# A hybrid decoder step on Trainium2: where the first output projection step stands beside the sample attention's tail

## The reference, cut to what matters

```
o   = softmax(q_lat . past_c + q_rope . past_r) . past_c      # per sample token and head: a latent of 256
a   = einsum('bshr,rhv->bshv', o, w_uv)                       # 8 heads of 64: 512 values a token
g   = spatial_gate(u, v, w_s, b_s)                            # 512 values a token
x   = x + concat(rmsnorm(a) * g_mla, rmsnorm(g) * g_gmlp) @ w_out
```

## Time and profile before

| | |
|---|---|
| time before, median of 3 runs | 1296.98 us (1295.57 to 1297.92) |
| the profiled execution's own time | 1297.65 us |
| its span | 1295.9 us |
| PE busy | 1259.2 us, 97% |
| PE weight loads busy | 1181.9 us, 91% |
| DVE busy | 903.9 us, 70% |
| ACT busy | 592.9 us, 46% |
| POOL busy | 559.1 us, 43% |
| granted PE clock, mean | 0.993 |

### The profile page before, as it was taken

How to read it: one execution, slowest core, us unless ns; L and a number is a source line. 1 busy time by engine, 2 the same in 40 slices (tenths; PEclk the granted TensorE clock), 3 DMA queues, 4 the chain that set the end, 5 groups by cost and what they waited for, 6 DMA issues and landing times.

```text
span 1295.9 us, 24153 instructions
## 1 busy us (share of the span) xinstructions
PE 1259.2 (97%) x9110; PEld 1181.9 (91%) x9110; DVE 903.9 (70%) x1470; ACT 592.9 (46%) x1222; POOL 559.1 (43%) x567
## 2 busy tenths in 40 slices
PE   9999999999999989999999999999999999999997
PEld 7888998888787559999899999999999999999987
DVE  4983167777765436188955787676776679899986
ACT  7433235665655324124454444444444544444462
POOL 0732344354431226751265977878877800000000
PEclk9999999999998999999999999999999999999998
DMA  9421102000027435630221222222222397868503
GB/s 324 144 63 34 49 5 76 5 21 1 17 70 269 156 145 201 204 119 26 84 83 60 92 74 78 90 70 92 85 75 92 122 339 262 295 196 267 164 1 139
DMA packets 70405, 151.93 MB, mean 117 GB/s; under 512 B 9138, under 2 KB 16690, under 8 KB 69842
## 3 DMA queue, kind: packets, MB, share of 16 engines
q1 hardware_dynamic: 70290, 150.39, 34.5%
HBM read 127.80 MB, written 22.56 MB: 116 GB/s over the span
## 4 chain that ended last, share of the span: by engine, by line
PE 79%; DVE 9%; issue 4%; ACT 3%; POOL 2%; DMA 2%; SPq 0%; DVEq 0%; POOLq 0%; ACTq 0%
PE ps L1196 23%; PE ps L1198 23%; PE ps L1197 23%; PE ps L1442 2%; DMA araw<-in_w_dn 1%; PE ps L1500 1%; PE ps L1454 1%; PE ps L1562 1%; PE ps L1455 1%; ACT pTH L1880 1%; DVE nmx L2735 1%; POOL chunk L1165 1%; DVE pTL L2752 1%; PE ps L1527 1%; DVE prob L2729 1%
## 5 line engine op out<-in xcount | busy, mean ns | idle before, releaser
L1165 POOL TENSOR_TENSOR chunk<-wraw,chunk 128x256 fp32r<-128x256 f32 x193 | 163.2, 869 | 100.0 <-ACT chunk L1880 99.9
L1196 PE MATMUL ps<-bHL,aHL 128*128 128x272 f32 x616 | 178.3, 289 | 2.7 <-DVE bHL L3283 2.7
L1198 PE MATMUL ps<-bHL,aHL 128*128 128x272 f32 x616 | 177.2, 288 | 0.0
L1197 PE MATMUL ps<-bHL,aHL 128*128 128x272 f32 x616 | 177.1, 288 | 0.0
L1165 POOL TENSOR_TENSOR chunk<-wsum,chunk 128x256 fp32r<-128x256 f32 x134 | 115.8, 881 | 26.7 <-ACT chunk L1880 26.5
L1880 ACT ACTIVATE chunk<-wraw 128x256 fp32r<-128x256 f32 x193 | 74.9, 412 | 104.7 <-PE ps L1198 38.4
L1196 PEld LDWEIGHTS ps<-bHL,aHL 128*128 128x128 f32 x616 | 116.0, 188 | 3.9 <-DVE bHL L3283 3.8
L1197 PEld LDWEIGHTS ps<-bHL,aHL 128*128 128x128 f32 x616 | 116.0, 188 | 0.0
L1198 PEld LDWEIGHTS ps<-bHL,aHL 128*128 128x128 f32 x616 | 115.9, 188 | 0.0
L1188 POOL TENSOR_TENSOR rt<-ms,mhalf 128x3 f32<-128x3 f32 (+1 forms) x3 | 4.4, 1463 | 246.1 <-DVE ms L3373 246.1
L1102 POOL TENSOR_TENSOR prob<-prob,rsm 128x128 f32<-128x128 f32 (+5 forms) x48 | 49.6, 1042 | 78.2 <-DVE rsm L2724 78.2
(11 more groups left out here) (494 smaller groups left out, 4605.1 us busy)
## 6 DMA issues: line engine op xcount, KB each, us to landing
araw<-in_w_dn SPq DMA_DIRECT2D x121, 256.0 KB, 3.2
wraw<-in_w_gu SPq DMA_DIRECT2D x44, 512.0 KB, 3.8
cp<-in_cache SPq DMA_DIRECT2D x64, 272.0 KB, 4.7
ab<-acts SPq DMA_DIRECT2D x34, 272.0 KB, 3.8
raw<-in_w_out SPq DMA_DIRECT2D x16, 512.0 KB, 4.3
acts<-bufC SPq DMA_DIRECT2D x22, 272.0 KB, 2.1
xt<-in_x_tok SPq DMA_DIRECT2D x9, 512.0 KB, 5.6
x<-x2s SPq DMA_DIRECT2D x8, 544.0 KB, 6.0
```

The lines of the kernel that those rows point to most:

```text
L1165: pool.tensor_tensor(x[:, 1, :], source_of(i, step), x[:, 0, :], ALU.subtract).then_inc(cw_lo, 1)
L1196: nc.tensor.matmul(out, wh, xh, start=start, stop=False, skip_group_check=onto)
L1197: nc.tensor.matmul(out, wh, xl, start=False, stop=False, skip_group_check=onto)
L1198: return nc.tensor.matmul(out, wl, xh, start=False, stop=stop, skip_group_check=onto)
```

## The change

PE's order becomes `sample_product(3)`, q = 0, `sample_latents(3)`, the matmuls with `uvr` (now the function `sample_values`), q = 1, the sum of squares, q = 2, the spread, q = 3. `sample_latents(g)` writes bank g and no longer g % 3. On ACT `mixed_high(0)` moves ahead of `move_sample_product(3)`; on DVE `mixed_low(0)` moves ahead of `move_latents(3)`. q = 0 waits for the copies of group 0 out of bank 0 (`o4`), and the wait for `a4_e`, which guards bank 2, stays at q = 2. No instruction that computes is added or taken away, and no transfer is moved.

```diff
@@ PE
             def sample_latents(g):
                 pe.wait_ge(o4_tok, g + 1)
-                if g == 3:
-                    pe.wait_ge(o4, KC)
                 for r in range(KC):
-                    last = nc.tensor.transpose(ps[:, g % 3, P * r:P * r + P], otok[:, g, P * r:P * r + P],
+                    last = nc.tensor.transpose(ps[:, g, P * r:P * r + P], otok[:, g, P * r:P * r + P],
                                                ident[:, :])
...
             sample_product(3)
-            sample_latents(3)
-            pe.wait_ge(o4, KC * DUOS)
-            pe.wait_ge(ld_uv_x, 16)
-            for h in range(H):
...
-            last.then_inc(a4, 1)
+            def sample_values():
+                pe.wait_ge(o4, KC * DUOS)
+                pe.wait_ge(ld_uv_x, 16)
+                for h in range(H):
...
+                last.then_inc(a4, 1)
@@ PE, the loop over OUT_STEPS, ahead of the step's matmuls
                 if q >= 4:
                     pe.wait_ge(w_free, q - 3)
+                elif q == 0:
+                    pe.wait_ge(o4, KC)
                 elif q == 1:
+                    sample_latents(3)
+                    sample_values()
+                elif q == 2:
                     sum_squares(J_N3 + NC - 1, 6, sqm, KG, CH[NC - 1][1])
-                elif q == 2:
                     pe.wait_ge(a4_e, 1)
@@ ACT
             move_sample_turned(3)
-            move_sample_product(3)
...
             mixed_high(0)
+            move_sample_product(3)
             act.wait_ge(a4, 1)
@@ DVE
             move_latents(2)
-            move_latents(3)
...
             mixed_low(0, range(2 * KG))
+            move_latents(3)
             mixed_low(1, range(2 * KG))
```

More of the change, by code:

```diff
@@ L1616, in _ @@
             sample_product(3)
-            sample_latents(3)
-            pe.wait_ge(o4, KC * DUOS)
-            pe.wait_ge(ld_uv_x, 16)
-            for h in range(H):
[L1621 to L1624, removed]
-            last.then_inc(a4, 1)
+            def sample_values():
+                pe.wait_ge(o4, KC * DUOS)
+                pe.wait_ge(ld_uv_x, 16)
+                for h in range(H):
+                    out = ps[VH * (h % 2):VH * (h % 2) + VH, 2, NS * (h // 2):NS * (h // 2) + NS]
+                    for r in range(KC):
+                        last = nc.tensor.matmul(out, uvr[:, r, VH * h:VH * h + VH], olat[:, r, NS * h:NS * h + NS],
+                                                start=r == 0, stop=r == KC - 1)
+                last.then_inc(a4, 1)
             def row_sum(bank, sources, i, o):
@@ L2828, in move_latents @@
                     out = olat[:, r, :].rearrange("p (h b t) -> p b h t", h=H, b=NB)[:, 2 * g:2 * g + 2, :, :]
-                    nc.vector.tensor_copy(out, ps[:, g % 3, P * r:P * r + P].rearrange(
+                    nc.vector.tensor_copy(out, ps[:, g, P * r:P * r + P].rearrange(
                         "p (b h t) -> p b h t", b=2, h=H)).then_inc(o4, 1)
```

## The result

| | before | changed |
|---|---|---|
| median, 7 runs each | 1296.98 us (1295.27 to 1299.54) | 1302.71 us (1301.76 to 1304.44) |
| profiled execution, own time | 1297.65 | 1304.13 |
| span | 1295.9 | 1302.4 |

The ratio is 1.0044, with a 95% interval of 1.0034 to 1.0053: slower by 5.7 us, where 4.0 was forecast. The ratios on record are not the quotients of the medians; here the two differ most.

The account below looks back on a forecast made before the run. PE, busy 97% of the span, was taken to bound the kernel. PE's order -0.65 + 0.53 + 2.78 = +2.66 plus the clock's 1.4 gave +4.1 on 1296.98, forecast 1301.0 us, range 1298.7 to 1303.0.

Parts of the forecast that it names:

- The wait for the product's copy goes: PE after the last sample product: its standing for ACT's copy disappears because q = 0 stands in its place, -0.65 us.
- q = 0 waits for its low operand: PE at q = 0: DVE's mixed_low(0) is held by POOL's weight splits, +0.53 us, bounds 0 and +1.2.
- q = 1 must wait for its operand: PE after the uvr matmuls: mixed_high(1) stands behind a4, copy and squares on ACT, +2.78 us, bounds 2.5 and 3.2.
- The clock: PE around q = 1: granted clock likelier than not falls to 1.2 GHz, +1.4 us, bounds 0 and 5.1.
- Rival (a): PE around q = 1: the clock does not fall; +2.7 us, 1299.7; chance 0.30.
- The sum of squares moves behind q = 1: PE ahead of q = 2: the sum of squares' 1.89 us is paid either way, so 0.
- The means, the power and the spread: DVE's means and power after the sum of squares: done 498.05, PE asks at 498.2; only just in time, up to +0.3.
- (b): Part of the slip is absorbed or overrated at q = 1's operand, DVE's hold or later PE waits; 1298.3; chance 0.12.
- (c): Faster: q = 0 hides ACT's copy and nothing waits at q = 1, as block 1's operand is ready; 1296.3; chance 0.06.
- (d): q = 0 is held until DVE is done at 484.5 and hides nothing; 1301.8; inside the forecast case's 0.52.

Follow-up runs that it names:

- e2: Changed kernel, but POOL splits the weights of i = 1 only after mixed_low(0) is done: 1301.13 us, ratio 1.0033 to the kernel before.
- e3: Changed kernel, but on ACT mixed_high(1) stands ahead of the wait for a4: 1297.74 us, ratio 1.0007 to the kernel before.
- e7: Changed kernel with 10 spare products by ones on PE after the uvr matmuls, ahead of q = 1: 1300.26 us, ratio 1.0028 to the kernel before.
- e6: Kernel before with only the ACT and DVE moves of mixed_high(0) and mixed_low(0), PE's order as before: 1302.04 us, ratio 1.0043 to the kernel before.
- e4: Changed kernel, but the sum of squares stands between the uvr matmuls and q = 1: 1299.50 us, ratio 1.0021 to the kernel before.
- after_again: Changed kernel run once more, unaltered, for its median and a second trace: 1300.67 us against 1297.22, ratio 1.0037 to the kernel before.
- e1: Changed kernel with 15 spare products by ones on PE after the uvr matmuls, ahead of q = 1: 1300.48 us, ratio 1.0027 to the kernel before.
- e8_latents_inside: Changed kernel, mixed_high(1) ahead of a4's wait, POOL's second split behind mixed_low(0), last group's transposes inside q = 0: 1295.12 us, ratio 0.9985 to before.

## Why the prediction was right

**The direction and the main mechanism were right, step by step.** Predicted and measured, in the changed kernel's first trace, from the start of the last product:

| step | predicted | measured |
|---|---|---|
| product to q = 0 | 3.60 | 3.60 |
| q = 0, partly held by DVE | 3.65 | 3.81 |
| transposes to `uvr` matmuls | 1.02 | 0.96 |
| `uvr` matmuls to q = 1 | 3.91 | 3.92 |
| q = 1 | 3.28 + 1.4 | 4.59 |
| sum of squares to q = 2 | 1.90 | 1.91 |
| sum | 18.76 | 18.79 |

That the sum agrees to 0.03 is in part luck: the second trace gave 18.66, and the terms of q = 0 and q = 1 erred by +0.16 and -0.09.

*The wait for the product's copy goes* (-0.65): shown, q = 0 starts 3.60 behind the product.

*q = 0 waits for its low operand*: +0.53 predicted, 3.81 - 3.11 = 0.70 measured, and in e2 q = 0 is back at 3.12. What the Trainium skill states of the port pair that DVE and GpSimd share ("SBUF — State Buffer", "SBUF: two separate sides"), an exclusive lock held for the whole instruction, agrees with the trace: three operations of DVE were each held by one of POOL's. POOL was held too, by 0.19 on w1H and 0.08 on w1L.

*q = 1 must wait for its operand*: +2.78, measured 2.72 of standing; e3 removes it and with it the loss.

*The clock*: +1.4, measured 1.2 (4.59 against e7's 3.38) and 1.1 in the second trace (4.44). The fall came in all four traces with 2.63 or 2.72 us of standing beside the `uvr` matmuls (the changed kernel twice, e2, e6), and in none of the other eight, where the longest such standing is e4's 1.77. The executions without a trace agree. Worked out from the granted clock of each, the means are 0.9916, 0.9929, 0.9922 and 0.9925 for the changed kernel twice, e2 and e6, and 0.9934 to 0.9945 for all the others; 3.4 us at 1.2 GHz lower the mean by 3.4 / 2 / 1300 = 0.0013. Rival (a) is ruled out.

Two things in this term came out well without being known. The prediction judged the fall by one execution of before, where it came 2.5 us after the first of the L1488 matmuls; over the twelve traces it came 2.3 to 5.2 us after it. And the price let the clock come back 3.5 us after q = 1 begins. It came back 3.3 and 3.0 us after q = 1's first matmul in the changed kernel, 4.2 in e2, and 3.4 after q = 0's in e6; what was alike in all four is the 3.4 us from the fall to the return. The price was near because the fall lay close to the start of q = 1.

*The sum of squares moves behind q = 1: 0* was off by 0.25. q = 2 now follows the sum of squares, and takes 501.51 - 498.26 = 3.25 where it took 3.00; the step after these matmuls pays for a slow first one (0.53 in place of 0.29). Before, q = 1 paid it: 489.13 0.53 stands in the earlier trace rows. In the changed kernel q = 1 is paced by DVE, and the 0.25 comes on top. Some 13 us behind q = 2's start the difference between the two first traces is still exactly 4.34: the same step begins 27.48 us after the product in before (505.19) and 31.82 in the changed kernel (511.29). The means, the power and the spread were in time, as worked out.

**The size of the whole was short by 1.7 us in the first comparison** (5.7 against 4.0). The stretch and the 0.25 make 4.34; the first interval begins at 4.4, and the second comparison's (2.7 to 6.9) holds it. The profiled spans differ by 6.50: 1.76 ahead of the last product, 4.09 in the stretch, 0.65 behind the start of q = 2, of which 0.25 are named. The 1.76 is not shown to be an effect of the change: `after_again` reached the same place at 474.25, 3.5 us earlier than before. Beyond the 0.25 no missing term of the sum is shown. What the runs do show is how far single executions differ: the mean granted clock of the seven changed executions was 0.9916 in the first comparison and 0.9929 in the second, which is 3.4 us more at 1.2 GHz and 1.7 us of time as an estimate, and the medians of the two sets differ by 2.0. The clocks of before's executions in the first comparison are not on record, so the excess stays open. So do the remaining 0.4 behind q = 2: from q = 2 to the end of the span it was 803.49 and 802.33 before, 804.14 and 803.49 in the changed kernel, and 802.3 to 804.5 over all twelve traces.

**The rivals.** (b), that a part is absorbed, is ruled out by the stretch behind q = 2, which gave nothing back. (c), faster, needed `mixed_high(1)` ahead of `a4`; e3 shows that this is the point that decides, and that even then the change gives only 0.15 us in the stretch and pays 0.25 behind it, since DVE's hold (0.70) takes back what the hidden wait gives (0.65). It needs e2's edit as well to gain. (d) did not occur: q = 0 began at once and was held only at its third group.

## What to carry to other kernels

When work is moved into a gap on the bounding engine, ask for the next step's operand too: an engine that splits operands in order must have issued the next block's split before it waits for a result that now comes later. Judge such a move in one stretch of the trace, from a fixed event ahead of it to one behind it, since whole executions scatter by more than the effect. And where PE must stand, a gap of some 2.7 us beside small matmuls cost another 1.1 to 1.5 by the clock, which spare matmuls, or better a piece of real work, avoid. The spare matmuls rest on two traces here (e1, e7), the real work on one (e4).

## What the runs showed of the hardware that was not expected

The spread of the kernel's times (1295.3 to 1299.5 before) has one source that the traces show: the granted clock is at 1.2 GHz for 3.4 to 10.2 us from 411.8 to 415.0 us on, during 32 matmuls of 64 rows and 64 columns (L1488) or up to 1.4 us behind them. The earliest and the latest start of the last product lie 5.2 apart (474.25 and 479.47); 1.2 of it stood already at the first of the L1488 matmuls (409.38 and 410.55), and 4.0 came behind it, where the low clock lasted 6.8 us longer (half of that, 3.4, is the clock's share as an estimate). A float32 product of 128x128 by ones on L1223 appears as two matmuls, 30 for 15 calls, at 0.12 us each. In e8_latents_inside, POOL's second split met DVE's `mixed_low(1)` in turn, whose first four operations took 3.10 in place of 1.74; PE waited for none of them.
